# Diagonal 32x32 and 64x64 block products in TensorE's column tiles for the gated-linear-attention levels, with refitted tables

## The reference, cut to what matters

```python
b = jnp.cumsum(gc, axis=1)
inter = jnp.einsum('bchk,bhkv->bchv', qc * jnp.exp(b), s)
rel = jnp.where(mask, b[:, :, None] - b[:, None, :], -jnp.inf)
attn = jnp.einsum('bihk,bjhk,bijhk->bhij', qc, kc, jnp.exp(rel))
intra = jnp.einsum('bhij,bjhv->bihv', attn, vc)
```

## Time and profile before

| what | value |
|---|---|
| runs, median (lowest to highest) | 1459.83 us (1456.72 to 1460.92), 3 runs |
| the profiled execution's own time | 1460.64 us |
| its span, first to last instruction | 1458.8 us |
| mean granted TensorE clock | 0.995 of full |
| busy share of the span | PE 97%, weight loads 92%, DVE 53%, POOL 48%, ACT 41% |

### The profile page before, as it was taken

One profiled execution on the slowest core, in us unless ns is written; L12 is line 12 of the kernel. 1 busy time (PEld: TensorE's weight loads), 2 busy tenths in 40 slices (PEclk: granted clock), 3 DMA queues, 4 the chain that ended last, 5 costly groups with the idle time before them and its releaser, 6 DMA issues.

```text
span 1458.8 us, 22483 instructions
## 1 busy us (share of the span) xinstructions
PE 1410.7 (97%) x9083; PEld 1336.0 (92%) x9083; DVE 774.5 (53%) x992; ACT 603.5 (41%) x836; POOL 701.6 (48%) x296
## 2 busy tenths in 40 slices
PE   6999999999999999999998999999989999999998
PEld 4888999998998999999978889999989899999998
DVE  4559978885864221210265798689858442211012
ACT  3553444454634333332246334445464443333231
POOL 1344444444463555555534444344436646555552
PEclk9999999999999999999999999999999999999998
DMA  9865333333543655553435633243335334434332
GB/s 333 285 212 165 102 87 102 109 102 101 201 138 114 210 176 173 174 191 129 130 99 169 211 119 103 83 123 102 101 102 202 122 123 132 130 123 123 129 117 72
DMA packets 163311, 208.65 MB, mean 143 GB/s; under 512 B 9228, under 2 KB 135176, under 8 KB 163208
## 3 DMA queue, kind: packets, MB, share of 16 engines
q1 hardware_dynamic: 162656, 207.00, 43.9%
q10 hardware_dynamic: 552, 0.22, 0.1%
HBM read 204.05 MB, written 3.15 MB: 142 GB/s over the span
## 4 chain that ended last, share of the span: by engine, by line
PE 76%; DVE 12%; ACT 4%; DMA 3%; issue 2%; SPq 1%; POOL 1%; DVEq 0%; ACTq 0%; POOLq 0%
PE ps L748 22%; PE ps L750 21%; PE ps L749 21%; DVE fac L1810 2%; DVE conv_acc L1676 1%; DMA w_raw<-in_w_in_dram 1%; DVE attn L1820 1%; PE ps L661 1%; ACT w_hi L1243 1%; POOL w_lo L621 1%; DVE h_lo L1641 1%; PE ps L792 1%; DVE fac L1792 1%; PE ps L793 1%; PE ps L794 1%
## 5 line engine op out<-in xcount | busy, mean ns | idle before, releaser
L621 POOL TENSOR_TENSOR w_lo<-w_raw,w_hi 128x1024 fp32r<-128x1024 f32 x288 | 698.1, 2425 | 734.3 <-ACT w_hi L1243 535.8
L748 PE MATMUL ps<-h_hi,w_hi 128*128 128x384 f32 x1600 | 546.9, 342 | 5.5 <-DVE h_lo L1641 3.8
L750 PE MATMUL ps<-h_hi,w_lo 128*128 128x384 f32 x1600 | 535.6, 335 | 0.0
L749 PE MATMUL ps<-h_lo,w_hi 128*128 128x384 f32 x1600 | 535.4, 335 | 0.0
L1243 ACT ACTIVATE w_hi<-w_raw 128x1024 fp32r<-128x1024 f32 x199 | 207.5, 1043 | 449.5 <-PE ps L750 304.1
L748 PEld LDWEIGHTS ps<-h_hi,w_hi 128*128 128x128 f32 x1600 | 300.6, 188 | 22.6 <-issue 12.1
L749 PEld LDWEIGHTS ps<-h_lo,w_hi 128*128 128x128 f32 x1600 | 300.9, 188 | 1.4
L750 PEld LDWEIGHTS ps<-h_hi,w_lo 128*128 128x128 f32 x1600 | 300.7, 188 | 0.0
L1676 DVE SCALAR_TENSOR_TENSOR conv_acc<-conv_in,cw,conv_acc 128x399 f32<-128x399 f32 x240 | 204.4, 913 | 1.8
L1538 ACT ACTIVATE w_hi<-w_raw 128x1024 fp32r<-128x1024 f32 x88 | 93.1, 1060 | 226.5 <-PE ps L750 177.9
L1996 DVE TENSOR_TENSOR sq<-sq,ps 128x768 f32<-128x768 f32 x22 | 21.0, 954 | 255.4 <-PE ps L750 255.4
(11 more groups left out here) (255 smaller groups left out, 1665.4 us busy)
## 6 DMA issues: line engine op xcount, KB each, us to landing
w_raw<-in_w_in_dram SPq DMA_DIRECT2D x112, 512.0 KB, 3.6
w_raw<-in_w_ffn_in_dram SPq DMA_DIRECT2D x88, 512.0 KB, 3.5
mod_late<-in_w_mod_dram SPq DMA_DIRECT2D x55, 512.0 KB, 5.4
w_raw<-in_w_ffn_out_dram SPq DMA_DIRECT2D x44, 512.0 KB, 3.7
mod_early<-in_w_mod_dram SPq DMA_DIRECT2D x32, 512.0 KB, 6.0
w_raw<-in_w_branch_dram SPq DMA_DIRECT2D x24, 512.0 KB, 3.4
w_raw<-in_w_out_dram SPq DMA_DIRECT2D x16, 512.0 KB, 3.4
mod_second<-in_w_mod_dram SPq DMA_DIRECT2D x9, 512.0 KB, 11.3
```

The source lines that it names most:

```text
L621: nc.gpsimd.tensor_tensor(m["w_lo"][:, n % SPL, cols], m["w_raw"][:, n % RAW, cols], m["w_hi"][:, n % SPL, cols].bitcast(F32), ALU.subtrac ...
L748: mm(out, hi[:, at:at + P], rhs[0][:, k, :], start=start, stop=False)
L749: mm(out, hi[:, at:at + P], rhs[1][:, k, :], start=False, stop=False)
L750: ins = mm(out, lo[:, at:at + P], rhs[0][:, k, :], start=False, stop=stop)
```

## The change

`product` no longer multiplies 128 by 128 for every level. With n = max(32, 2^(i+1)) it forms only the n x n blocks along the diagonal, each with its own weight load of n columns and its own n moving columns, into partitions b to b + n of PSUM. Levels 0 to 4 get four 32x32 products per old one, level 5 two of 64x64, level 6 stays. The level of plain queries with keys (i < 0) and the two `whole` steps stay. The tables are set anew: SP issues some `mod_early` loads earlier, PE multiplies the last four of those blocks one piece group earlier, one gate-vector load in layer 0 comes after piece 5 in place of 6, ACT copies the GLA output two pieces earlier, and the convolution taps are shared out a little differently.

```diff
-GATE_LOAD = [5, 5, 5, 5, 6, 7, 8, 8]
+GATE_LOAD = [5, 5, 5, 5, 5, 7, 8, 8]
 GATE_AT = [4, 6, 6, 6, 6, 7, 7, 8]
-EARLY_LOAD = [7, 8, 8, 9, 9, 14, 15, 15, 15, 16, 16, 18, 18, 21, 21, 22]
-EARLY_AT = [11, 11, 11, 11, 11, 12, 12, 13, 16, 16, 16, 16, 17, 17, 18, 18]
+EARLY_LOAD = [7, 8, 8, 9, 9, 14, 15, 15, 15, 15, 15, 17, 17, 19, 20, 21]
+EARLY_AT = [11, 11, 11, 11, 11, 12, 12, 13, 16, 16, 16, 16, 16, 16, 17, 17]
...
-GLA_HI_ACT = 42
+GLA_HI_ACT = 40
...
-LEVEL_TAPS = [0, 2, 8, 7, 4, 7, 7]
-STATE_TAPS = 15
-OUT_TAPS = [5, 6, 6, 2]
-MAX_TAPS = [1, 2, 2, 1, 2, 3, 1, 2, 0, 4, 5, 1]
-WEIGHT_TAPS = [2, 5, 3, 0, 6, 3, 2, 6, 6, 2, 6, 8]
+LEVEL_TAPS = [0, 2, 8, 7, 2, 7, 7]
+STATE_TAPS = 17
+OUT_TAPS = [6, 6, 6, 2]
+MAX_TAPS = [1, 2, 2, 1, 2, 3, 1, 2, 0, 3, 5, 1]
+WEIGHT_TAPS = [2, 5, 3, 0, 6, 3, 2, 6, 8, 2, 6, 8]
...
-                        f = f"fac{i % 2}"
-                        return mm(out, part(f, 1, hh, tt), part(f, 0, hh, tt), start=True, stop=True)
+
+                        keys, queries = part(f"fac{i % 2}", 1, hh, tt), part(f"fac{i % 2}", 0, hh, tt)
+                        n = max(32, 2 << i)
+                        for b in range(0, P, n):
+                            ins = mm(out[b:b + n, b:b + n], keys[:, b:b + n], queries[:, b:b + n], start=True, stop=True)
+                        return ins
```

## The result

| what | before | after |
|---|---|---|
| runs, median (lowest to highest) | 1460.24 us (1456.72 to 1461.41), 10 runs | 1465.06 us (1460.10 to 1469.46), 10 runs |
| the profiled execution's own time, span | 1460.64, 1458.8 us | 1461.16, 1459.4 us |
| mean granted TensorE clock in it | 0.995 | 0.992 |

The ratio is 1.0037 with a 95% interval of 1.0022 to 1.0052: slower, where faster was forecast, and outside the range. The profiled execution is 3.9 us shorter than the median of its kernel, so the trace shows only part of the loss. The ten runs' mean granted clock lies between 0.987 and 0.992, lower in the longer ones; the two runs at the median have 0.989. As an estimate, 0.003 less in the mean is 8.8 us more at half the clock, and so 4.4 us less of PE's work: the size of those 3.9 us. No trace shows where they lie.

What follows compares the result with a forecast made beforehand. DVE was taken to set the pace through levels 3 to 6, PE behind them. Per layer 0 (level 0's saving) + 1.1 (taps) + 1.4 (POOL) = 2.5 us, two layers 5.0 us, gave 1454.8 us; range 1450 to 1461.5 us.

Steps and rivals of the forecast that it cites:

- What bounds the kernel: Two regimes: DVE sets the pace through levels 3 to 6, PE behind them; what counts is how much sooner level 6 starts.
- The products themselves: A level's products on PE take 0.8 us (0.6 to 1.3) in place of 1.54, saving 0.75; level 5 saves 0.6.
- one-by-one issue: Rival: small products on PE issue at 57 ns per pair, levels 0 to 4 take 5.5 us each, 1501 us; chance 0.08.
- The moved modulation blocks: After piece 16 PE waits 1.7 us, hidden, for load 13; SP's piece 20 queues behind it; the exponential of level 4 ends at 130.7.
- level 0's saving: DVE's stretch begins 0.75 us sooner (1.35 in layer 1); taken as lost at multiply(4): 0, between -0.75 and +3.
- Slower by SP's queue: Rival: load 13 takes 7.3 us, multiply(4) comes 3.0 us later, 1463.6 us; decides from a landing of about 5.4; chance 0.10.
- The taps: Two convolution taps fewer on DVE before multiply(6), where four take 2.27 us: 1.1 us per layer saved, on the path.
- POOL beside DVE: In build(6) a DVE exponent instruction waits 2.2 us beside a POOL subtraction; 1.4 us of that taken as freed.
- another such meeting: Bound of the POOL term: a further DVE wait beside a POOL subtraction, up to 2.4 us, against 2.2 us freed.
- Everything counts: Rival: DVE's stretch shrinks by 5 us, PE becomes the bound and gains some 5 to 6 a layer, 1449.8 us; chance 0.10.
- A level 6 held by PE: Sign that the forecast is wrong in kind; it had PE at level 6 about 155.0, in time for a start about 155.9.

Runs made afterwards that it cites:

- g1: e3 with the changed kernel's new EARLY_LOAD (issue of the modulation loads) alone; PE multiplies the blocks where it did before: 1471.27 us, ratio 1.0065.
- f5: The changed kernel with level 4 after piece 18 in place of 17: 1466.41 us, ratio 1.0030 to the kernel before.
- h3: f2 with DVE copying level 5 before multiply(6), and two taps moved from ahead of multiply(6) to behind it: 1466.75 us, ratio 1.0027.
- f1: The changed kernel with load 13 issued behind weight piece 20 (loads 14 and 15 behind piece 21): 1458.28 us, ratio 0.9976 to the kernel before.
- e3: The changed kernel with both modulation tables (EARLY_LOAD, EARLY_AT) as before, all else as changed: 1458.37 us, ratio 0.9989 to the kernel before.
- e1: The kernel before with the block products alone, every table old: 1457.56 us, ratio 0.9984 to the kernel before.
- f2: e3 with level 4 after piece 18 in place of 17: 1453.52 us, ratio 0.9950 to the kernel before.
- h1: The kernel before, with its 128x128 products and all its tables, and level 4 alone moved behind piece 18: 1458.88 us, ratio 0.9978.
- g2: f2 with level 6 after piece 22 in place of 21 as well: 1460.17 us, ratio 0.9994 to the kernel before.
- h2: e3 with 8 idle-filling products, never read, in front of level 4's wait: 1463.79 us, ratio 1.0012 to the kernel before.
- f4: e3 with 12 idle-filling products, never read, in front of level 4's wait: 1462.03 us, ratio 1.0003 to the kernel before.

## Why the prediction was wrong, by its own steps

**What bounds the kernel** held: wherever DVE became later (g1, f5) or its order was disturbed (h3), PE waited for it at the next step that needs it.

**The products themselves** were well sized: 0.97 us against 0.8 per level, 0.89 for level 5, both inside the bounds. 96 pairs start within 0.94 us, 9.8 ns each, so the rival of one-by-one issue is out. By the Trainium skill's rule ("TensorEngine Tiling (Array Packing)", Instruction Overhead), as an estimate, a level of such products one behind the other would be 2.4 us; for products spread over row halves and column tiles this trace disagrees, and the measurement decides. In layer 1, level 0 takes some 1 us (2.86 before), but the slow clock then lies on the piece behind it: up to the modulation group it is 6.80 us in place of 7.48, 0.68 saved of the 1.35.

**The moved modulation blocks** is the step that failed: "I take level 0's saving as lost here: 0". Measured, multiply(4) came 2.75 us later in layer 0 and 3.05 in layer 1, of which 0.94 and 1.13 lie ahead of level 0: +1.8 and +1.9 us where the sum has 0. The chain was the right one, and its times were too early. The exponential of level 4 was to end at 130.7; it ended at 134.16, 3.46 later. That is 0.94 by which the whole execution ran later at level 0; 1.6 because the group after piece 16 started 35.16 us behind level 0 and not 33.57 (a level saves 0.57, not 0.75, and block 6 waited 1.2 us for its load, which I hadn't looked for); 0.2 until product 8 was done; and 0.8 because piece 20, on its way together with load 13, reached ACT 5.69 us after that load's issue and not 4.9 (rounding and exponential overlap by 0.1, which comes off). The 3.5 us of a load was the row of before; after, the weight pieces issued in the same window take 5.0 us:
```profile
w_raw<-in_w_in_dram SPq DMA_DIRECT2D x4, 512.0 KB, 5.0
```
Only the step's first half held: PE's wait, forecast at 1.7 us and measured at 2.15, is indeed nearly free (f1).

So the mechanism of the rival *Slower by SP's queue* is what happened. That its 1463.6 us is near the 1465.06 measured is luck: its condition, a load of 7.3 us, didn't come, and the profiled execution shows little of the loss. I gave it 0.10, because its deciding point was misplaced: it looked at load 13's landing alone (3.8 us at most, far below 5.4), while the 1.1 us of slack could be eaten just as well by a later product 8 and by piece 20's own landing. The spread of my own bound, -0.75 to +3, said as much, and I took 0 of it.

**The taps**: the two taps take 1.18 us instead of 2.27, as costed, and copy_level(5) follows multiply(4) 1.3 us sooner. At the end no gain shows: e3 has the taps and e1 hasn't, and their ratios differ by 0.05%, inside both intervals.

**POOL beside DVE** failed as a sum, not at the place that it named. The instruction of 2.77 us takes 0.55 now (L1797 at 153.24), so all of its 2.2 us were freed. But multiply(4), late, starts beside POOL's subtraction of piece 20 (132.92) and takes 2.73 us in place of 1.74; the second exponent instruction (L1796) takes 0.65 us more in build(5) and 0.33 more in build(6); and a meeting that the forecast had left out of its sum stays, 2.65 us at 147.99 and before:
```profile
143.57 2.63 DVE L1789 TENSOR_TENSOR fac<-prefix 128x384 f32<-128x384 f32 x1
```
From multiply(4) to copy_level(5) 1.27 us are won, 1.1 by the taps and 0.2 here, not 1.4: the bound "another such meeting" was the better guess. Together, a start 2.75 us late and 1.2 not won make 155.9 into 159.87, where level 6 came. (*Everything counts* has a slip of its own: its terms for PE add up to 6.6 us, not 5 to 6; nothing hangs on it.)

**The half clock** was missing from the sum. I had used the row at 802.4 only to price level 0. All around DVE's stretch PE's savings turned into longer waits, and behind these stood half-clock stretches. By the prediction, PE that "only arrives sooner at a DVE that isn't ready" costs nothing; but of the 7.0 us of work that PE was spared its busy time fell by 3.1 only, and e1's piece 18, 6.49 us instead of 4.10, shows one place where the rest went. In layer 1 it decides: copy_level(5) starts at 872.21, 0.97 later than before and no later than level 0 was, but PE, at 0.61 behind its wait of 1.31 us for level 4, comes to level 6 only at 875.40. A level 6 held by PE was the forecast's own sign of being wrong in kind.

## What to carry to other kernels

When a load is moved earlier on an in-order queue, list what stands behind it and when each of those is needed: the price isn't the load's own wait, but the lateness of the first thing queued behind it that the pacing engine needs. Work saved on an engine that then waits is worth only part of itself: of 7.0 us the block products gave 2.6 with the old tables (e1), and some 4.1 with level 4 moved by one piece (f2 against h1); the difference between the two is not clear of the noise. Moving on to the next wait, without asking what it feeds, gave all of it back (g2, h3).

## What the runs showed of the hardware

96 products of 32x32 over 64 rows, with 96 weight loads, start within 0.94 us, 48 of 64x64 within 0.83. The granted clock stood at 0.50 to 0.53 behind waits of PE of 2.15 us (the changed kernel), 2.35 (e1) and 2.56 (e3), not behind the 1.72 us of before, and not always: 2.35 us at product 13 in f1's layer 1, and 2.44 and 2.53 us for the merged branches in h2's and f4's layer 0, were followed by pieces at 1.00. So a wait of one length may or may not bring a slow stretch, and the mean granted clock differs from run to run of one kernel (0.987 to 0.992 after). Taps, multiplies and exponent instructions that fall beside a subtraction of POOL take up to 2.82, 2.75 and 2.77 us in place of 0.62, 1.75 and 0.55; none of the 42 copies of a level does (0.71 to 0.76 us each, before and after).
